# Segments of 512 columns in the middle state pass, batched halo terms, and row-wise claims for residual loads

## What is computed

```python
h = rmsnorm(x); u_pool, u_rnn, u_gate, g_pool, g_rnn = split(h @ w_in)
y_pool = pool_mixer(u_pool) @ w_pool_out              # trailing windows 2/4/8/16
v = conv4(u_rnn)                                      # y_t = b + sum_k w[k] * u_{t-3+k}
r, i = sigmoid(v @ w_a + b_a), sigmoid(v @ w_x + b_x) # 8 diagonal blocks of 128
a = exp(-8 * r * softplus(-lam)); b = sqrt(1 - a*a) * i * v
s_t = a_t * s_{t-1} + b_t                             # along the sequence
y_rnn = (s * gelu(u_gate)) @ w_rnn_out
x = x + (sigmoid(g_pool) * y_pool + sigmoid(g_rnn) * y_rnn) @ w_o
g, u = split(rmsnorm(x) @ w_ffn_in); x = x + (silu(g) * u) @ w_ffn_out
out = rmsnorm(x)
```

## Time and profile before

| | us |
|---|---|
| time, median of 3 runs | 1113.86 |
| the 3 runs | 1180.95, 1113.86, 1113.6 |
| time of the profiled execution | 1112.0 |
| span of its slowest core (core 6) | 1110.4 |
| spans of the even cores 0, 2, 4, 6 | 1109.8, 1108.0, 1104.9, 1110.4 |
| spans of the odd cores 1, 3, 5, 7 | 1075.6, 1074.1, 1078.5, 1080.5 |
| busy on core 6: PE, DVE, ACT, POOL | 995.2, 727.9, 473.7, 257.5 |

### The profile page before, as it was taken

The page is one execution under the profiler, slowest core; times in us unless marked ns, Lnnn a source line. Parts: engine busy times, 40 slices in busy tenths (PEclk is TensorE's granted clock), DMA queues, the critical chain, the costliest instruction groups (busy, mean ns, idle before and its releaser), DMA issues.

```text
span 1110.4 us, 18573 instructions; the slowest of 8 cores (1074.1 to 1110.4 us)
## 1 busy us (share of the span) xinstructions
PE 995.2 (90%) x4720; PEld 444.9 (40%) x4720; DVE 727.9 (66%) x840; ACT 473.7 (43%) x602; POOL 257.5 (23%) x394
## 2 busy tenths in 40 slices
PE   3996679998879998798999999979999799999996
PEld 2442234443334443343444444434444344444442
DVE  4569777588997547987658989893633433334336
ACT  3476764256645216656228747761211110110112
POOL 4221423141352201431113404220101120120201
PEclk9998899999999999989999999989999899999998
DMA  8973459786316722436355726855146562461623
GB/s 219 178 137 75 109 113 212 209 192 143 67 23 151 151 58 48 67 69 127 91 169 117 125 86 214 214 147 152 61 145 152 99 114 36 77 104 25 109 39 155
DMA packets 64914, 132.65 MB, mean 119 GB/s; under 512 B 7200, under 2 KB 11680, under 8 KB 64800
## 3 DMA queue, kind: packets, MB, share of 16 engines
q0 software_dynamic: 29232, 52.05, 30.2%
q1 hardware_dynamic: 35568, 79.32, 21.9%
HBM read 162.40 MB, written 20.97 MB: 165 GB/s over the span
## 4 chain that ended last, share of the span: by engine, by line
PE 72%; DVE 13%; issue 8%; ACT 4%; DMA 1%; POOL 1%; DVEq 0%; SPq 0%; ACTq 0%; POOLq 0%
PE ps L815 52%; PE ps L1160 13%; DVE f_v_f L857 4%; PE ps L1105 3%; PE ps L760 2%; PE ps L885 2%; DVE R_f L857 1%; DVE f_v_f L862 1%; DMA X<-x 1%; DVE R_f L941 1%; DVE f_w_f L928 1%; POOL rs_f L750 0%; PE ps L1029 0%; DVE ACW_f L857 0%; ACT hbt_f L744 0%
## 5 line engine op out<-in xcount | busy, mean ns | idle before, releaser
L815 PE MATMUL ps<-H_f,ring_f 128*128 128x512 bf16 x2816 | 649.0, 387 | 31.2 <-DVE uh_f L866 8.4
L815 PEld LDWEIGHTS ps<-H_f,ring_f 128*128 128x128 bf16 x2816 | 274.2, 99 | 385.9 <-issue 86.5
L1135 ACT ACTIVATE th_f<-ps 128x512 f32<-128x512 f32 (+1 forms) x66 | 48.7, 739 | 225.1 <-PE ps L815 220.0
L1160 PE MATMUL ps<-ACW_f 128*128 128x512 bf16 x528 | 116.4, 379 | 0.0
L676 POOL DMA_DIRECT2D ring_f<-w_ffn_in x88 | 47.3, 538 | 288.7 <-PE ps L815 244.0
L1139 DVE SCALAR_TENSOR_TENSOR th_f<-th_f,ps 128x512 f32<-128x512 f32 (+1 forms) x66 | 57.0, 864 | 80.0 <-ACT th_f L1135 62.7
L857 DVE SCALAR_TENSOR_TENSOR f_v_f<-ps,par,f_v_f 128x511 f32<-128x511 f32 (+5 forms) x90 | 89.6, 996 | 25.2 <-ACT f_v_f L852 16.6
L748 POOL TENSOR_SCALAR ms_f<-ms_f 128x1 f32<-128x1 f32 x64 | 23.5, 367 | 244.2 <-ACT hbt_f L744 241.6
L1045 ACT ACTIVATE th_f<-ps 128x512 f32<-128x512 f32 (+1 forms) x48 | 35.2, 738 | 101.8 <-PE ps L815 93.8
L1160 PEld LDWEIGHTS ps<-ACW_f 128*128 128x128 bf16 x528 | 51.4, 98 | 61.5 <-issue 0.4
L1166 DVE SCALAR_TENSOR_TENSOR X<-ps,X 128x1024 f32<-128x1024 f32 x36 | 43.9, 1223 | 41.9 <-PE ps L1160 37.3
(11 more groups left out here) (129 smaller groups left out, 1137.3 us busy)
## 6 DMA issues: line engine op xcount, KB each, us to landing
ring_f<-kept SPq DMA_DIRECT2D x108, 256.0 KB, 3.0
ring_f<-w_ffn_in POOLq DMA_DIRECT2D x88, 256.0 KB, 4.1
xs<-x SPq DMA_DIRECT2D x24, 512.0 KB, 4.3
kept<-ring_f SPq DMA_DIRECT2D x44, 256.0 KB, 4.4
ACW_f<-w_ffn_out POOLq DMA_DIRECT2D x44, 256.0 KB, 4.4
X<-x SPq DMA_DIRECT2D x20, 512.0 KB, 5.8
ring_f<-w_in POOLq DMA_DIRECT2D x36, 256.0 KB, 4.9
out<-X SPq DMA_DIRECT2D x12, 512.0 KB, 3.5
```

The source lines that it names most:

```text
L815: it.add(c_pe(n), lambda e, kc=kc, lo=lo, n=n, b=b: e.matmul(PS[pv.idx // 2][:, pv.idx % 2 + b, 0:n], lhsT=ring[:, w.idx, kc, :], rhs=src[ ...
L1135: it.add(c_act(U), lambda e, U=U, pg=pg, tv=tv: e.activation(out=two(th[:, tv.idx, 0:U], U), in_=P2(pg, U), func=AF.Tanh, scale=0.5), (pg, ...
L1160: it.add(c_pe(), lambda e, c=c, i=i: e.matmul(PS[pv.idx // 2][:, c, :], lhsT=acs[i][0](t * 128, (t + 1) * 128), rhs=WA[:, i, c * 512:(c + ...
```

## The change

1. **Halo terms.** The host puts a 3 by 3 matrix of convolution weights for each channel into `params` (from column `C_HALO`, 72 columns more). `halo_terms` computes, on POOL with three instructions for four blocks at a time, the three numbers `hc` that the next segment's first three columns lack. In `rnn_unit` one DVE add of three columns stands for the three instructions at L862, and the copy into `uh` goes from the end of the DVE item to the front of the ACT item. A batch is put into the graph when its fourth block is; a unit reads whichever batch was put last before it. In the middle pass, where blocks 0 and 1 of both segments of a group come before blocks 2 and 3 of the first, the first three columns of blocks 0, 1, 4 and 5 of a group's second segment therefore get terms of an earlier batch.
2. **Claims.** A residual load of c1b claims the two rows of R that its tile covers.
3. **Middle pass.** For role 0 `((1024,), (1024,))` becomes `((512, 512), (512, 512))`: two groups of two segments, each weight block still loaded once for a group. `more` goes from (4, 2, 4, 2) to (3, 3, 3, 3), `deep` from true to false.
4. **Numbers of the planner**, for both roles. Among them: role 0 `dev` 2 to 1, `devt` 2 to 0 (these copies go to ACT), `pmo` 3 to 0, `pbo` 0 to 2, `pbt` 2 to 0, `pao` 1 to 0, `pat` 0 to 1, `B1` 386.59 to 603.44; role 1 `devt` 2 to 1, `pbo` 4 to 2, `pao` 4 to 0, `pat` 3 to 1, and the last pair of c0 split. The sequences of c0 change.
5. Code that can put extra matmuls into idle stretches. It acts only when `keep` is in the numbers of a role, and it is in neither.

```diff
--- before.py
+++ after.py
@@ -32,19 +32,19 @@
         self.tune = tune
 
 
-TUNE0 = {"seq": "g0 g1 c01 g23 g45 c23 c45 g67 c67", "nc0": -3.85, "nc0s": 3.0, "step": 24.05, "gelu": 4.32,
-         "halo": 43.21, "pool": 25.05, "pools": 0.39, "t1": 93.39, "t1s": 1.88, "B0": 73.78, "S0": 285.6,
-         "B1": 386.59, "S1": -3.62, "B2": 589.89, "S2": 304.97, "ahead": 22.26, "c1": 1.278, "m": 37.56, "f": 7.53,
-         "u": 7.799, "slack": 0.098, "dev": 2, "hs": 20.8, "devt": 2, "pvo": 1, "pvt": 4, "pmo": 3, "pmt": 0,
-         "pbo": 0, "pbt": 2, "pao": 1, "pat": 0}
-TUNE1 = {"seq": "p0 p1 p23 g01 c01 p45 g23 c23 p67 g45 c45 g67 c67", "nc0": 11.68, "nc0s": 3.0, "step": 20.24,
-         "gelu": 3.77, "halo": 34.0, "pool": 45.93, "pools": 7.44, "t1": 183.82, "t1s": -0.44, "B0": 154.25,
-         "S0": 122.17, "B1": 334.63, "S1": -4.81, "B2": 394.66, "S2": 261.45, "ahead": -59.77, "c1": 0.565,
-         "m": 29.63, "f": 14.85, "u": 2.664, "slack": 0.121, "dev": 0, "hs": 20.01, "devt": 2, "pvo": 4, "pvt": 1,
-         "pmo": 1, "pmt": 0, "pbo": 4, "pbt": 0, "pao": 4, "pat": 3}
+TUNE0 = {"seq": "g0 g1 c01 g2 g3 g45 c45 c23 g67 c67", "nc0": -2.46, "nc0s": -2.59, "step": 29.08, "gelu": 17.26,
+         "halo": 38.76, "pool": 23.05, "pools": 0.39, "t1": 93.39, "t1s": 1.88, "B0": 64.72, "S0": 266.39,
+         "B1": 603.44, "S1": -5.59, "B2": 605.34, "S2": 238.8, "ahead": 31.99, "c1": 1.297, "m": 24.67, "f": 11.3,
+         "u": 6.552, "slack": 0.099, "dev": 1, "hs": 19.39, "devt": 0, "pvo": 1, "pvt": 4, "pmo": 0, "pmt": 0,
+         "pbo": 2, "pbt": 0, "pao": 0, "pat": 1}
+TUNE1 = {"seq": "p0 p1 p23 g01 c01 p45 g23 c23 p67 g45 c45 g67 c6 c7", "nc0": 11.68, "nc0s": -1.2, "step": 22.79,
+         "gelu": 1.4, "halo": 34.0, "pool": 47.28, "pools": 7.44, "t1": 236.41, "t1s": -0.44, "B0": 201.28,
+         "S0": 122.17, "B1": 334.63, "S1": -4.1, "B2": 394.66, "S2": 245.88, "ahead": -59.66, "c1": 0.611,
+         "m": 35.5, "f": 14.85, "u": 1.297, "slack": 0.121, "dev": 0, "hs": 21.04, "devt": 1, "pvo": 4, "pvt": 1,
+         "pmo": 0, "pmt": 0, "pbo": 2, "pbt": 0, "pao": 0, "pat": 1}
 
 ROLES = (
-    Role(0, (), 1024, ((1024,), (1024,)), (512, 512), 512, 5, (4, 4, 4, 4), (8, 8, 8, 8), (4, 2, 4, 2), True, 3, 4, True, TUNE0),
+    Role(0, (), 1024, ((512, 512), (512, 512)), (512, 512), 512, 5, (4, 4, 4, 4), (8, 8, 8, 8), (3, 3, 3, 3), False, 3, 4, True, TUNE0),
     Role(1024, (1024,), 1024, (), (512, 512), 512, 5, (4, 4, 4, 4), (8, 8, 8, 8), (0, 0, 0, 0), False, 3, 4, True, TUNE1),
 )
 OWN = 2048
@@ -53,7 +53,8 @@
 
 
 C_CW, C_CB, C_BA, C_BX, C_LAM, C_PS, C_INV = 0, 32, 40, 48, 56, 64, 68
-C_N = 68 + 64
+C_HALO = 68 + 64
+C_N = C_HALO + 72
 
 
 class _Op:
...
@@ -602,14 +605,15 @@
 
         XR = R[:, :, :].rearrange("p k n -> p (k n)").bitcast(F32)
         ACP = PM[:, :, :].rearrange("p k n -> p (k n)")[:, 0:8 * NB].rearrange("p (m n) -> p m n", m=8)
-        RALL = [("R", j, q) for j in range(8) for q in range(2)]
+        RW = R[:, 0, :].shape[1]
         PALL = [("PM", j, q) for j in range(4) for q in range(2)]
 
         def xtile_of(seg, t):
 
             if seg != "c1b":
                 return (lambda: X[:, t * D:(t + 1) * D]), xtile(t), xtile(t)
-            return (lambda: XR[:, t * D:(t + 1) * D]), [("XR", t)], [("XR", t)] + RALL
+            return (lambda: XR[:, t * D:(t + 1) * D]), [("XR", t)], [("XR", t)] + [
+                ("R", j, q) for j in range(t * 2 * D // RW, -(-(t + 1) * 2 * D // RW)) for q in range(2)]
 
         def ac_of(seg, i):
 
@@ -837,6 +841,22 @@
         SQ = []
         gel = {}
 
+        halo_done = {}
+
+        def halo_terms(j0, p):
+
+            js = range(j0, j0 + 4)
+            mat = par[:, C_HALO + 9 * j0:C_HALO + 9 * j0 + 36].rearrange("p (j i m) -> p j i m", j=4, i=3)
+            it = Item("pool", p, "halo")
+            it.add(0.6, lambda e: e.tensor_tensor(
+                out=hx[:], in0=mat, in1=uh[:, j0:j0 + 4, :].unsqueeze(2).to_broadcast([128, 4, 3, 3]), op=ALU.mult),
+                [("uh", j) for j in js] + ["par"], ("hx",))
+            it.add(0.5, lambda e: e.tensor_tensor(out=hc[:, j0:j0 + 4, :], in0=hx[:, :, :, 0], in1=hx[:, :, :, 1],
+                                                  op=ALU.add), ("hx",), [("hc", j) for j in js])
+            it.add(0.5, lambda e: e.tensor_tensor(out=hc[:, j0:j0 + 4, :], in0=hc[:, j0:j0 + 4, :], in1=hx[:, :, :, 2],
+                                                  op=ALU.add), ("hx",), [("hc", j) for j in js])
+            G.put(it)
+
         def rnn_unit(seg, j, w, p):
             U = SEG[seg][1]
             tag = "r" + seg
@@ -849,6 +869,9 @@
             pu, v = psv(U), fval("v")
             hproj(pu, w, seg, p + T["u"], tag + ".u", also=(v, "rnnseq"), early=(seg == first and j == 0), contig=True)
             it = Item("act", p, tag + ".v0")
+            if seg != "c1b":
+                it.add(0.22, lambda e: e.activation(out=uh[:, j, :], in_=flat(pu, U)[:, U - 3:U], func=AF.Copy),
+                       (pu,), (("uh", j),))
             it.add(c_act(U, 2), lambda e: e.activation(out=F(v)[:, 0:U], in_=flat(pu, U), func=AF.Identity,
                                                        scale=cp(C_CW, 24 + j), bias=cp(C_CB, j)), (pu, "par"), (v,))
             G.put(it)
@@ -858,13 +881,13 @@
                     out=F(v)[:, d:U], in0=flat(pu, U)[:, 0:U - d], scalar=cp(C_CW, 8 * (3 - d) + j), in1=F(v)[:, d:U],
                     op0=ALU.mult, op1=ALU.add), (pu, "par"), (v,))
             if seg != first:
-                for d in (1, 2, 3):
-                    it.add(0.17, lambda e, d=d: e.scalar_tensor_tensor(
-                        out=F(v)[:, 0:d], in0=uh[:, j, 3 - d:3], scalar=cp(C_CW, 8 * (3 - d) + j),
-                        in1=F(v)[:, 0:d], op0=ALU.mult, op1=ALU.add), (("uh", j), "par"), (v,))
+                it.add(0.25, lambda e: e.tensor_tensor(out=F(v)[:, 0:3], in0=F(v)[:, 0:3], in1=hc[:, j, :], op=ALU.add),
+                       (("hc", j),), (v,))
+            G.put(it)
             if seg != "c1b":
-                it.add(0.17, lambda e: e.tensor_copy(out=uh[:, j, :], in_=flat(pu, U)[:, U - 3:U]), (pu,), (("uh", j),))
-            G.put(it)
+                halo_done.setdefault((seg, j // 4), []).append(j)
+                if len(halo_done[(seg, j // 4)]) == 4:
+                    halo_terms(j // 4 * 4, p)
             vb = Val("vb")
             if on_pool("pv", seg, j):
                 it = Item("pool", p, tag + ".vb")
@@ -1320,7 +1343,44 @@
                 else:
                     res.append(k)
             return res
+
+        KEEP = T.get("keep", 0.0)
...
+        done_by = {}
+        for it in order:
...
             for fn, rd, wr in it.ins:
                 sem = it.dma
                 if sem == "ring":
@@ -1331,6 +1391,7 @@
                 def call(e, fn=fn, vals=[(v, v.idx) for v in it.vals]):
                     return fn(e)
                 o = S.op(it.eng, call, phys(rd), phys(wr), dma_sem=sem)
+                done_by[id(it)] = o
                 o.common = it.prio if it.tag in ("idn", "g1", "par") or any(it is x for x in XL[:TCOMMON]) else None
 
         S.finalize()
@@ -1465,6 +1526,11 @@
     base[:, C_BX:C_BX + 8] = chan(f(b_rg_x)[0])
     base[:, C_LAM:C_LAM + 8] = chan(f(lru_lambda)[0])
     base[:, C_PS:C_PS + 4] = chan(f(pool_scale)[0])
+    halo = np.zeros((128, 8, 3, 3), np.float32)
+    for i in range(3):
+        for m in range(i, 3):
+            halo[:, :, i, m] = cwp[:, 8 * (m - i):8 * (m - i) + 8]
+    base[:, C_HALO:C_HALO + 72] = halo.reshape(128, 72)
     first = ROLES[0].first
     in_maps = []
     for c in range(8):
```

35 lines of the change are left out of this document (added).

## The result

| | before | after |
|---|---|---|
| time, median | 1113.98 us | 1079.24 us |
| the runs | 1113.6 to 1180.95 | 1075.83 to 1080.61 |
| ratio, 95% interval | | 0.9685 (0.9653 to 0.9716) |

What follows compares the result with a forecast made beforehand. Even cores set the time, PE waiting behind a nearly full DVE in c1 and for PSUM in the middle. Core 6: 1110.4 - 6.5 - 8 - 9 - 2 = 1084.9, plus 1.6 and 1.9, gives 1088 us; range 1066 to 1110.

Steps and rivals of the forecast that it cites:

- the forecast's own case: Whole kernel: the summed gains hold, ending at 1088 us, own range 1078 to 1098; chance 0.52.
- the third rival: Odd cores end last: middle and c0 give 25 us or more, even cores reach 1070; some 1070, chance 0.12.
- The claims, -6.5: c1b's last residual tiles: row-wise claims let four loads go together, -5.5 us, plus about 1 from clock.
- DVE's order holds the last tile: c1b's residual tiles: the bound at which the claims change nothing, 0 us, DMA being the other possible cause.
- The c1 stage, -8: c1 stage: 12.0 us less DVE work lets PE stall less, -8 us, bounds -3 and -14.
- with DVE clearly below PE, half of the 16 us excess should go: c1 stage: PE's time above its floor, 16 us, halves once DVE is lighter, giving the -8.
- about 2 us more: c1 stage: b products leaving POOL shorten DVE's own instructions through the shared port, about 2 us, left out.
- The middle, -9: Middle pass: 512-column units free PSUM earlier, 10 us back less 1 to 2 for ACT; bounds -25 and +56.
- DVE ... +7 over 370 us, bare nowhere: Middle pass: doubled units add 18 us of DVE, less 10.9 for transposed tiles; +7, all hidden.
- PSUM ... the bank is free after the third tap: no halo steps and no copy ahead of the release: Middle pass: earlier release of a unit's input bank returns half of some 20 us PE idle, 10 us.
- ACT, +68 and no bound: Middle pass: shorter units, table loads and tiles add 68 us of ACT, not full on average.
- c0, -2: c0 stage: copy gone from the release of eight banks, -2 us, between -8 and +8; new sequence unpriced.

Runs made afterwards that it cites:

- the coarse claim: Changed kernel, order kept, but each c1b residual load waits as if it wrote all of R: 1081.28 us, ratio 0.9704.
- b_fine_claims: Kernel before, order kept, only the dependency tracker hears the row-wise claims of the residual loads: 1113.93 us, ratio 0.9996.
- a_dve_time: Changed kernel, order kept, plus three small DVE instructions on a scratch tile in each of 48 halo units: 1116.02 us, ratio 1.001.
- a_halo_dve: Changed kernel, order kept, old halo repair and `uh` copy back on DVE, POOL batches and ACT copy left out: 1116.28 us, ratio 1.0025.
- a_dve_time_release: Changed kernel, order kept, three small DVE instructions per halo unit, the last reading the unit's PSUM input bank: 1116.84 us, ratio 1.0026.
- a_old_numbers_mid1024: Kernel before plus halo batches and row-wise claims, middle in 1024-column segments, all planner numbers old, planned anew: 1117.61 us, ratio 1.0034.
- a_old_numbers: Changed kernel's halo, claims and 512-column segments with all old planner numbers of both roles: 1115.51 us, ratio 1.0025.
- a_old_priorities: Changed kernel's structure and new engine split, with old priorities and sequences, planned anew: 1107.97 and 1108.73 us in two executions, no ratio.

## Why the prediction was right, and where it was off

**The direction and the cores: right, the sum with luck.** 1079 is inside the range, by the forecast's own case (1078 to 1098) at its lower edge. But the two larger of its four terms were off and made up for each other in part: c1, set at 8 us, gave nothing, and the middle, set at 9, gave 25. The odd cores stayed 28 us away, though not as forecast: they were to end near 1075 and their spans are 1043 to 1046. The even cores did come down to the 1070 at which the third rival had the odd ones end last; only the odd ones' own gain, 37 us on core 7 where that rival had priced some 14, kept them out of the way.

**The claims, -6.5: right, in part by the order.** SP's waits for R tiles are gone, and the last add follows its matmuls. Alone and planned anew they give 5.4 (6.6 in the end), and in the change the end gains 7.8, of which the coarse claim takes back 2.6 to 3.7. At the place itself the step is nearly exact: from the end of the w_o matmuls to PE's long run of FFN matmuls it was 13.4 us (857.8 to 871.17) and is now 8.3 (822.59 to 830.86), 5.1 less for the 5.5 forecast, and the stalls left there are under a microsecond and a half each. The bound's lower end, "DVE's order holds the last tile", is what b_fine_claims showed at 0.

**The c1 stage, -8: the lighter DVE came, the gain did not.** DVE's busy time fell by 12.6 (154.4 to 141.8) against 12.0 forecast. PE's lost time stayed: 20.9 to 20.7 on core 0, 20.2 to 20.6 on core 6, outside the bounds of -3 and -14. So the step "with DVE clearly below PE, half of the 16 us excess should go" failed. It is true that more DVE time costs here: 12.8 us in a_dve_time, 10.7 in a_halo_dve. But less of it did not pay by itself: with the new split and the old priorities the stage loses 36.1, with all old numbers 23.3, or 34.4 with 1024 columns. With the old halo the new order stands at 31.4 here, 10.5 worse than before, and the lighter DVE gives that back and no more; why the order costs it, no run shows.

The b products on DVE took 0.711 to 0.723 where 0.746 had been set. Before, with POOL doing every second one, they took 0.973 on average: from their starts and ends in the trace of core 6, the five with no POOL instruction beside them took 0.68, the other three 1.46. The 512-column scans took 1335 ns, and now 1286 with POOL 6 us less busy in that window; the taps, which read PSUM, took 0.745 to 0.748 with or without POOL beside them. The page SBUF — State Buffer of the Trainium skill, section SBUF: two separate sides, has it that a DVE operation with two SBUF inputs and a GpSimd operation hold one port pair exclusively; these rows agree. Of the about 2 us more that the prediction named beside its sum some 1.3 are there: 16 x 0.03 for b against the 0.746 of the sum, and 16 x 0.05 for the scans.

**The middle, -9: this is the term that was mis-sized, 25 measured.** Two sentences of it failed. "DVE ... +7 over 370 us, bare nowhere" looked at the share, 75%, and concluded that DVE's time was free. It fell by 6 instead of growing by 7 (275.88 to 270.05), and a_dve_time shows that it is not free: two thirds of the scratch instructions lie in the middle, 35 us of DVE's queue by the rows, and PE loses 23 there. And "PSUM ... the bank is free after the third tap: no halo steps and no copy ahead of the release" named the release as what comes back; a_dve_time_release puts the release at 0.8 us, or with what its shorter copy hides at some 4, of 37. The rows named after L866 in the earlier trace rows, on which I had leaned, do go away, but they were mostly the mark of a late DVE queue and not of a bank that is read late: the copy was the last of seven instructions in its item, and PE is as late in a_dve_time, where nothing reads the bank after the taps.

How the 25 divide is shown only in part. The halo's small instructions took 26.0 us of core 6's DVE queue in the middle and take 8.6 now, each counted from the end of the instruction before it; at the 0.7 of a_dve_time that would be 12 us, an estimate. The rows of the kernels planned anew fit it: on core 0 the middle goes from 43.5 to 31.5 with halo and claims alone (a_old_numbers_mid1024), to 25.0 with segments of 512 (a_old_numbers) and to 18.9 with the new numbers. But the first two pay it all back in c0 and c1, so these are places where time can be won, and not what each part is worth. With the old halo in the order of the change, the middle would have gained nothing (a_halo_dve, 45.2 against 43.5).

**ACT, +68 and no bound: right.** It grew by 78 (53 in the middle), with 14 more table loads of up to 16, each 1.283. The page ScalarE: Activation LUTs of the Trainium skill, section What ACT_TABLE_LOAD costs, would have each switch at 2.66 us; here 25 loads have 0.5 us of idle before them in all, and no load of core 6 has more than 0.02 behind it, so the trace again does not bear that out.

**c0, -2: small and off.** It gained 4.5 and 6.9, within the -8 to +8 that had been left to it. The old numbers on the new structure lose 26 us there (62.6 against 36.7), so this stage depends on order more than any other, as its missing rows had suggested.

**What stays open.** The forecast treated the numbers of the planner as a list of moved operations, and priced only those; the runs say that the priorities are worth 29 us with the new split, and 4 with the old. Which of them does it, and what in DVE's queue it changes, was not settled: a_old_priorities loses 13 in the middle and 15 in c1 with busy times within 3 us of the change on PE, DVE and POOL and 10 less on ACT. The split also moves work between ACT and POOL, so that it acts through DVE alone is argued. Nor was it shown that the segments of 512 columns are needed for the gain.

## What to carry to other kernels

Where an order is fixed in advance, price small instructions on an in-order engine by the queue time that they take, gaps included, and count most of it (0.7 to 0.8 here) even at 75% busy, if PE runs dry behind that engine anywhere in the stage. That holds for time added to a given order; time taken away pays only with an order that uses it, as c1 shows. Before a stage is given a gain, look whether a stall lies at its mark: one that moves across it looks like a gain of several microseconds. A wait that is removed pays only with an order that uses it: here 0 with the old one, 5.4 with a new one. Judge a lighter engine and the order of its queue as one edit, since each alone was worth about a fifth or less of the two together.

## What the runs showed of the hardware

- A three-column instruction costs about what its kind costs and not its size: an add 163 ns, a copy from PSUM 159, a multiply-add 221 to 234, each on DVE with 0.1 us ahead of it; on ACT a copy 170. A 12-column add on POOL took 208 at the median, 414 on average and up to 1287.
- The scratch multiply-add of a_dve_time took 325 on average, but no single one did: 67 of the 96 took about 0.22 us and 29 took 0.52 to 1.07. All of those 29 had POOL's cast of v running beside them, which becomes ready just then; of the 67 short ones on core 0, 47 had no POOL computation beside them. In a_halo_dve, where the cast follows the small instructions, 143 of 144 took 0.22.
- The mean granted clock of core 6 rose from 0.969 to 0.979, in the middle from 0.96 to 0.98: with shorter gaps in PE less of its work runs at the lower of its two levels, and a part of the middle's gain is that.
